# Seven block products for three pairs of feed-forward groups per stage

## The chip, the cores and the metric

The kernel runs on one core of one Trainium2 chip, as one program. The metric is the device time in microseconds: the median of three runs was 724.07 us (723.87 to 724.22). In the profile TensorE is PE (its weight loads PEld), VectorE is DVE, ScalarE is ACT, GpSimd is POOL and SyncE, which issues most DMAs, is SP.

## The reference

Two transformer-like blocks run one after the other on 256 tokens of width 1024, all in float32. The first block has a gated linear recurrence and a block-causal attention; the second has a Fourier and convolution mixer, a pooling mixer, and after each of the two a gated feed-forward part. The change is in that part alone, which is computed twice (layer 0 and layer 1, called the first and second feed-forward stage here):

```python
def swiglu_ffn(h, w_gate, w_up, w_down):
    return (jax.nn.silu(h @ w_gate) * (h @ w_up)) @ w_down
# h: 256 x 1024, w_gate and w_up: 1024 x 2816, w_down: 2816 x 1024
x = x + swiglu_ffn(rmsnorm(x, norm_ffn_g_2[layer]), ...)
```

## The kernel before

**Numbers.** Each float32 operand of a big product is split into a high part in the format fp32r and the rest as a low part. `product` (L1638) then does three matmuls into one PSUM bank: high by high, high by low, low by high. Weights come from memory in slabs of 128 x 2048 floats (1 MB). For a slab, ScalarE copies the raw slab into the high part (`stream`, L665) and VectorE subtracts that from the raw slab to get the low part (L1068 is the helper that records every such two-operand instruction). There are five raw buffers and four split buffers (`NRAW`, `NSPL`).

**Tiling.** The 2816 hidden columns are 11 groups of 256. For a group i, gate and up columns stand side by side, 512 columns; two slabs cover the 8 blocks of 128 input rows (kt 0 to 3, kt 4 to 7). `gate_up` (L2042) does, for both halves a of the tokens (128 each) and 8 kt, three matmuls of 512 columns: 48. ScalarE applies silu with the row norm to the gate half (`gates`, L1002), VectorE multiplies it with the up half (`hidden`, L1071). TensorE turns the result (`turn_hidden`, four 128 x 128 transposes, L2064), ScalarE and VectorE split it (`hidden_high`, `hidden_low`), and `down` (L2068) multiplies it with one slab of w_down: 24 matmuls into four banks that are held for the whole stage.

**Order.** It is written by hand, one list for each engine, and each engine runs its list in order. TensorE's unit for group i is gate and up of i, turn of i − 1, down of i − 2. ScalarE and VectorE run their share of `stream` three slabs ahead of TensorE: `fill(k)` (L682, L1122) brings them to slab k + 3 (`LOOK`). A split buffer is free for slab k when TensorE is done with slab k − 4 (`before_split`, L525). The unit's list on both is: fill of its two slabs, gates or hidden of both token halves, the split of the turned group i − 1, fill of the down slab. The four remaining PSUM banks go round in a ring between gate and up results and turned groups. SyncE issues a slab's DMA when the raw buffer's slab five ahead of it has been split (`emptied`).

Of the kernel before, what the change touches and what calls it, by code (L numbers as in the profile page):

```python
# [6 lines left out]
P, T, D, KT = 128, 256, 1024, 8  # L7
# [5 lines left out]
STEPS = [step for i in range(NG) for step in [("gu", i)] + ([("d", i - 2)] if i >= 2 else [])]  # L13
STEPS += [("d", NG - 2), ("d", NG - 1)]
# [3 lines left out]
def slab_plan():  # L18
# [45 lines left out]
    for layer in range(2):  # L64
        if layer:
            plan.append(("heads", "pool_map_2", 0))
        for kind, i in STEPS:
            if kind == "gu":
                plan.extend(("gu", None, layer, k0, i) for k0 in (0, 4))
            else:  # L70
                plan.append(("down", "ffn_w_down_2", layer, i))
# [28 lines left out]
RING = [i for i in range(len(PLAN)) if i not in OWN]  # L100
MATS = [i for i in RING if PLAN[i][0] not in ("first", "mod")]
# [15 lines left out]
def slab_of():  # L117

    at, k = {}, 30
    for layer in range(2):  # L120
        if layer:
            at["pool"] = k
            k += 1
        for kind, i in STEPS:
            at[kind, layer, i] = k
            k += 2 if kind == "gu" else 1
    assert k == len(MATS)
    return at


AT = slab_of()


# [34 lines left out]
def outputs():  # L168
# [100 lines left out]
    for layer in range(2):  # L269
        held("d", layer)  # L270
        ring = 0

        def take(*names):
            nonlocal ring
            for x in names:
                o.place(4 + ring % 4, x)
                ring += 1

        for i in range(NG):
            two = run("gu", (layer, i, 0), (layer, i, 1))  # L280
            take(*two)
            if i == 0:
                turned(2 * layer, 1)
            o.finish(*two)
            o.slab(AT["gu", layer, i], None)
            o.slab(AT["gu", layer, i] + 1, two[1])
            if i:
                take(("ht", layer, i - 1))
                o.finish(("ht", layer, i - 1))
            if i >= 2:  # L290
                o.slab(AT["d", layer, i - 2], None)
        take(("ht", layer, NG - 1))
        o.finish(("ht", layer, NG - 1))
# [21 lines left out]

OUT = outputs()
# [20 lines left out]
def two_block_program(nc, w_d, vec_d, cst_d, dft_d, rcnt_d, row_d, x_d, out_d):  # L337
# [6 lines left out]
    with ctx:  # L344
# [17 lines left out]
        F0 = sb("f0", [P, 8 * 272])  # L362
        F1 = sb("f1", [P, 8, T])
# [34 lines left out]
        s_sum = {k: sem(f"s_sum{k}") for k in BY_DMA}  # L398

# [57 lines left out]
        prow, frow = acc[0], acc[1]  # L457

# [62 lines left out]

        def raw_of(i):
            return raw[RING.index(i) % NRAW]

# [9 lines left out]
        def freed(name):  # L534
# [38 lines left out]
            if kind == "gu":  # L573
                return s_hid, hid_at(*at)
            if kind == "ht":
                return s_glo, NG * i + at[1] + 1
# [6 lines left out]
        def hid_at(layer, i, a):  # L583
            return 2 * (NG * layer + i) + a + 1
# [4 lines left out]
        def _(e):  # L589
# [5 lines left out]
            n_mod = n_mat = 0  # L595
            emptied = []
            for i, slab in enumerate(PLAN):
                n = width(i)
                if i in OWN:
# [12 lines left out]
                else:  # L612
                    n_mat += 1
                    k = n_mat - 1
                    emptied.append((s_minus, BY_DMA.index(k) + 1) if k in BY_DMA else (s_lo, LOW_AT[k]))
                    if n_mat == 6:
# [9 lines left out]
        def _(e):  # L626
# [27 lines left out]
            e.dma_start(rc, rcnt_d).then_inc(s_rc, 16)  # L654
            e.dma_start(prow[:, :], row_d[0]).then_inc(s_prow, 16)
            e.wait_ge(s_cv3, 1)
            e.dma_start(frow[:, :], row_d[1]).then_inc(s_frow, 16)

        @block.scalar
        def _(e):  # L660
# [6 lines left out]
            def stream(upto):  # L667

                while at["plan"] <= upto:
# [6 lines left out]
                    p.wait_ge(*landed(i))  # L676
# [319 lines left out]
            def gates(layer, i):  # L996
                for a in range(2):
                    at_ = hid_at(layer, i, a)
                    p.wait_ge(*ended("gu", layer, i, a))
                    if at_ > 4:  # L1000
                        p.wait_ge(s_hid, at_ - 4)
                    e.activation(tt[(at_ - 1) % 4][:, :], bank_of("gu", layer, i, a)[:, 0:T], ACT.Silu,  # L1002
                                 scale=rn[:, 2 * layer, a:a + 1]).then_inc(s_sgt, 1)

# [9 lines left out]
            def ffn(layer):  # L1014
# [12 lines left out]
                for i in range(NG):  # L1027
                    k = AT["gu", layer, i]
                    fill(k)
                    fill(k + 1)  # L1030
                    gates(layer, i)
                    if i:
                        hidden_high(layer, i - 1)
                    if i >= 2:
                        fill(AT["d", layer, i - 2])
                hidden_high(layer, NG - 1)
# [26 lines left out]
        def _(e):  # L1063
# [41 lines left out]
            def stream(upto):  # L1105

                while at["plan"] <= upto:
# [12 lines left out]
                    tt_(w[:, 1, 0:n], raw_of(i)[:, 0:n], w[:, 0, 0:n].bitcast(f32), SUB).then_inc(s_lo, 1)  # L1120

# [423 lines left out]
            def hidden(layer, i):  # L1545
                for a in range(2):
                    at_ = hid_at(layer, i, a)
                    p.wait_ge(s_sgt, at_)
                    if i >= 2:
                        p.wait_ge(*ended("ht", layer, i - 2))  # L1550
                    stt(tt[4 + (at_ - 1) % 4][:, :], bank_of("gu", layer, i, a)[:, T:2 * T], rn[:, 2 * layer, a:a + 1],
                        tt[(at_ - 1) % 4][:, :], MUL, MUL).then_inc(s_hid, 1)

# [7 lines left out]
            def ffn(layer, *name):  # L1561
# [5 lines left out]
                for a in range(2):  # L1567
# [10 lines left out]
                for i in range(NG):  # L1578
                    k = AT["gu", layer, i]
                    fill(k)  # L1580
                    fill(k + 1)
                    hidden(layer, i)
                    if i:
                        hidden_low(layer, i - 1)
                    if i >= 2:
                        fill(AT["d", layer, i - 2])
                hidden_low(layer, NG - 1)
# [43 lines left out]
        def _(e):  # L1631
# [450 lines left out]

            def ffn(layer):
# [153 lines left out]
```

## Time and profile before

| | |
|---|---|
| median of three runs | 724.07 us |
| the profiled execution, its own time | 724.69 us |
| span in the profile (first to last instruction) | 722.9 us |
| mean granted TensorE clock | 0.994 of full speed |
| the two feed-forward stages, by the profile's times | about 329 to 515 us and 531 to 717 us |
| matmuls of 512 columns, mean of one (they overlap) | 389 to 395 ns, 1776 of them |
| slab splits: ScalarE copies, VectorE subtractions | 99 of 1913 ns, 95 of 2290 ns |
| HBM read | 156.74 MB |

The times of groups are busy times; matmuls overlap, so that the spacing of two of them is less than the duration of one. "Idle before" is the time in which the engine stood still ahead of an instruction, and the name behind the arrow is what ended it.

### The profile page before, as it was taken

What the parts mean: (1) busy time and instruction counts of PE and PEld (TensorE: products, weight loads), DVE (VectorE), ACT (ScalarE), POOL (GpSimd) and SP (SyncE); (2) the same over time, 40 slices, a digit from 0 to 9 for tenths busy, and PEclk for the clock granted to TensorE, in tenths of its full rate; (3) what the DMA queues carried; (4) which work ended last, traced back from release to release, by engine and by line L of the source; (5) the groups of instructions that cost most, each with busy time, mean ns of one, the idle gap of its engine ahead of it and who ended that gap; (6) DMA issues with size and microseconds to landing.
All of it is one profiled execution on the core that took longest, in us unless ns stands there. A gap on an engine that the chain in (4) does not pass through costs nothing.

```text
span 722.9 us, 9536 instructions
## 1 busy us (share of the span) xinstructions
PE 709.7 (98%) x3812; PEld 617.6 (85%) x3812; DVE 498.4 (69%) x799; ACT 397.1 (55%) x616; POOL 12.6 (2%) x18
## 2 busy tenths in 40 slices
PE   6999999999999999999999999999999999999996
PEld 5888889989999999888888888888888888888885
DVE  5789999798977889976754545545776455454544
ACT  3156536965775778778634444344755433444323
POOL 0000000000310001000000000000000000000000
PEclk8999999999999999999999999999999999999999
DMA  8999997599836359434755454555236554555101
GB/s 329 418 421 413 422 403 262 172 392 349 342 118 233 118 175 263 145 117 174 289 178 181 189 205 181 175 178 194 95 123 234 200 200 174 178 195 206 63 1 58
DMA packets 23469, 158.40 MB, mean 219 GB/s; under 512 B 2625, under 2 KB 2881, under 8 KB 5249
## 3 DMA queue, kind: packets, MB, share of 16 engines
q1 hardware_dynamic: 22464, 152.82, 56.4%
q0 software_dynamic: 960, 4.98, 2.5%
q8 instruction: 30, 0.49, 0.3%
q14 instruction: 15, 0.11, 0.0%
HBM read 156.74 MB, written 1.05 MB: 218 GB/s over the span
## 4 chain that ended last, share of the span: by engine, by line
PE 84%; DVE 9%; ACT 5%; DMA 1%; issue 1%; SPq 0%; DVEq 0%
PE pb L1640 21%; PE pb L1642 21%; PE pb L1641 21%; PE pb L1712 14%; DVE raw L1071 3%; DVE w L1068 3%; PE pb L1959 2%; PE pb L2064 1%; PE pb L2132 1%; ACT w L665 1%; PE pb L1987 1%; DMA x<-x_dram 1%; ACT t L783 1%; ACT r L780 1%; DVE r L1068 1%
## 5 line engine op out<-in xcount | busy, mean ns | idle before, releaser
L1068 DVE TENSOR_TENSOR w<-raw,w 128x2048 fp32r<-128x2048 f32 x95 | 216.9, 2290 | 142.8 <-ACT w L665 142.7
L665 ACT ACTIVATE w<-raw 128x2048 fp32r<-128x2048 f32 x99 | 188.5, 1913 | 144.6 <-PE pb L1642 114.7
L1640 PE MATMUL pb<-w,r 128*128 128x512 f32 (+1 forms) x608 | 238.8, 393 | 0.2 <-DVE r L1068 0.2
L1642 PE MATMUL pb<-w,r 128*128 128x512 f32 (+1 forms) x608 | 235.5, 387 | 0.0
L1641 PE MATMUL pb<-w,r 128*128 128x512 f32 (+1 forms) x608 | 235.0, 387 | 0.0
L1642 PEld LDWEIGHTS pb<-w,r 128*128 128x128 f32 x608 | 114.1, 188 | 23.8
L1640 PEld LDWEIGHTS pb<-w,r 128*128 128x128 f32 x608 | 114.2, 188 | 22.9 <-DVE r L1068 0.6
L1641 PEld LDWEIGHTS pb<-w,r 128*128 128x128 f32 x608 | 114.3, 188 | 22.3
L1640 PE MATMUL pb<-r,w 128*128 128x256 f32 x288 | 82.5, 287 | 0.3 <-DVE r L1068 0.3
L1642 PE MATMUL pb<-r,w 128*128 128x256 f32 x288 | 81.5, 283 | 0.0
L1641 PE MATMUL pb<-r,w 128*128 128x256 f32 x288 | 81.5, 283 | 0.0
L1071 DVE SCALAR_TENSOR_TENSOR raw<-raw,acc 128x1024 f32<-128x1024 f32 x64 | 75.1, 1219 | 4.4 <-DMA raw<-w_dram 4.4
L1712 PE MATMUL pb<-h,ow 128*128 128x256 f32 x256 | 56.6, 383 | 0.1
L1640 PEld LDWEIGHTS pb<-r,w 128*128 128x128 f32 x288 | 55.2, 192 | 0.8 <-DVE w L1068 0.7
L1712 PEld LDWEIGHTS pb<-h,ow 128*128 128x128 f32 x256 | 49.2, 193 | 7.4 <-issue 0.6
L1641 PEld LDWEIGHTS pb<-r,w 128*128 128x128 f32 x288 | 55.2, 192 | 0.1
L1642 PEld LDWEIGHTS pb<-r,w 128*128 128x128 f32 x288 | 55.2, 192 | 0.0
L1002 ACT ACTIVATE t<-pb,rn 128x256 f32<-128x256 f32 x44 | 20.7, 476 | 59.7 <-PE pb L1642 59.6
L1071 DVE SCALAR_TENSOR_TENSOR f<-f,vec 128x256 f32<-128x256 f32 x114 | 45.9, 476 | 0.1
L1071 DVE SCALAR_TENSOR_TENSOR t<-pb,rn,t 128x256 f32<-128x256 f32 x44 | 21.1, 482 | 22.8 <-ACT t L1002 22.8
L1712 PE MATMUL pb<-t,ow 128*128 128x256 f32 x128 | 27.8, 379 | 0.0
L1712 PEld LDWEIGHTS pb<-t,ow 128*128 128x128 f32 x128 | 24.3, 190 | 3.3
(215 smaller groups left out, 668.3 us busy)
## 6 DMA issues: line engine op xcount, KB each, us to landing
raw<-w_dram SPq DMA_DIRECT2D x129, 1024.0 KB, 4.9
ow<-w_dram SPq DMA_DIRECT2D x8, 1024.0 KB, 16.2
ow<-w_dram SPq DMA_DIRECT2D x8, 512.0 KB, 17.2
oh<-w_dram SPq DMA_DIRECT2D x2, 1024.0 KB, 22.1
w<-w_dram POOLq DMA_DIRECT2D x2, 1024.0 KB, 14.3
x<-x_dram SPq DMA_DIRECT2D x2, 512.0 KB, 5.7
f<-rc_dram POOLq DMA_DIRECT2D x1, 1024.0 KB, 5.1
acc<-row_dram POOLq DMA_DIRECT2D x2, 512.0 KB, 4.7
```

The source lines that it names most:

```text
L665: return e.activation(out, in_, ACT.Copy, **kw)
L780: e.activation(hi_of(R, kt), F3[:, kt, :], ACT.Identity, **kw).then_inc(done, 1)
L783: e.activation(tt[kt][:, :], F3[:, kt, :], ACT.Identity, **kw).then_inc(done, 1)
L1002: e.activation(tt[(at_ - 1) % 4][:, :], bank_of("gu", layer, i, a)[:, 0:T], ACT.Silu, scale=rn[:, 2 * layer, a:a + 1]).then_inc(s_sgt, 1)
L1068: return e.tensor_tensor(out, a, b, op)
L1071: return e.scalar_tensor_tensor(out, a, s, b, op0, op1, **kw)
L1640: e.matmul(out, a_hi, b_hi, start=start, stop=False)
L1641: e.matmul(out, a_hi, b_lo, start=False, stop=False)
L1642: return e.matmul(out, a_lo, b_hi, start=False, stop=stop)
L1712: return e.matmul(out, slab[:, o:o + P], rhs, start=start, stop=stop)
L1959: done = e.matmul(out_of("cv", 3), dg[j % 8], G0[:, 3, j:j + T], start=j == 0, stop=j == 30)
L1987: done = e.transpose(bank_of("tx", n, a, m)[:, j * P:j * P + P], Xt[:, a, o:o + P], ident)
```

## The change

Groups 3 and 4, 6 and 7, 9 and 10 of each stage are computed in pairs by Winograd's form of Strassen's scheme: the tokens are cut into two halves, the 1024 input columns into two halves, and the two groups are the two halves of the columns, so that 8 block products become 7. Each product is a half of the input rows by 512 columns for 128 tokens, 4 kt of three matmuls: 12 matmuls.

- Weights: the seven right sides are B11 (slab `11`), B21 (slab `21`) and five that VectorE forms. `form_sums` adds raw slabs of 128 x 2048 in place: B11+B12 (`e`), that + B22 (`g`), B12+B22 (`f`), and `g` + B21 (`h`); `22` is B22 itself. Slab 11 is loaded into a tile of its own, `chain` (F2's place), in which e, g and h follow. Each of the seven is split like a slab. As many slabs are loaded as before.
- Left sides: per stage, VectorE forms four blocks of the normed input (`block_sides`, `block_mixes`), ScalarE and VectorE split them (`block_high`, `block_low`) into the tile MX, which lies over F0 and F1.
- Results: ScalarE copies product 11 out (`snap`), and VectorE makes the two groups' four token halves from the products by seven sums of 128 x 512 (`made_from`: c11, u2, t, u3, c22, c12, c21). Gates and hidden of a pair read these sums, in the order (i, first half), (i+1, second), (i+1, first), (i, second).
- TensorE's order in a pair (`two_groups`): 11, 21, e, turn of i − 1, g, down of i − 2, f, 22, down of i − 1, h. In the last pair h stands ahead of the down of i − 1, and both groups are turned in the middle of that down. After an inner pair, the next single group turns both groups in the middle of its own gate and up.
- The matrix for the pooling mixer (rc, 1 MB) is loaded by GpSimd's queue after the last h of the first stage, since F2 is `chain` until then.

```diff
+PAIRS = (3, 6, 9)
+UNITS_OF = [("two" if i in PAIRS else "one", i) for i in range(NG) if i - 1 not in PAIRS]
+SEVEN = ("11", "21", "e", "g", "f", "22", "h")
+LAST = [NG - 2, NG - 1] if UNITS_OF[-1][0] == "two" else [NG - 1]
+SUMS = ("c11", "u2", "t", "u3", "c22", "c12", "c21")
...
+            plan.append(("11", None, layer, 0, i))
+            plan.append(("part", None, layer, 0, i + 1))
+            plan.append(("21", None, layer, 4, i))
+            plan.append(("part", None, layer, 4, i + 1))
+            plan.extend(("form", name, layer, i) for name in ("e", "g"))
+            plan.append(("down", "ffn_w_down_2", layer, i - 2))
+            plan.extend(("form", name, layer, i) for name in ("f", "22"))
+            rest = [("down", "ffn_w_down_2", layer, i - 1), ("form", "h", layer, i)]
+            plan.extend(rest if i + 2 < NG else reversed(rest))
...
+            seven = {name: ("seven", layer, i, name) for name in SEVEN}
+            r0, r1, r2, r3 = ring
+            for name, bank in zip(SEVEN, (r0, r1, r2, r0, r1, r3, r0)):
+                if name == "g":
+                    o.place(r3, *hts)
+                    o.finish(*hts)
+                o.place(bank, seven[name])
+                o.finish(seven[name])
+                o.slab(AT[name, layer, i], seven[name])
+            o.slab(AT["d", layer, i - 2], None)
+            o.slab(AT["d", layer, i - 1], None)
+            ring[:] = [r2, r1, r3, r0]
...
+        def emptied_at(i):
+
+            kind, name, layer, *at_ = PLAN[i]
+            if kind == "part":
+                return s_lo, LOW_AT[AT["f" if at_[0] == 0 else "22", layer, at_[1] - 1]]
+            if kind == "21":
+                return form_made("h", layer, at_[1])
+            k = MATS.index(i)
+            return (s_minus, BY_DMA.index(k) + 1) if k in BY_DMA else (s_lo, LOW_AT[k])
...
+                        p.wait_ge(s_lo, LOW_AT[AT["h", slab[2], PAIRS[q % len(PAIRS) - 1]]])
+                    e.dma_start(chain, w_d[i, :, :]).then_inc(s_ch, 16)
+                    continue
...
             e.wait_ge(s_flo, 4)
-            e.dma_start(rc, rcnt_d).then_inc(s_rc, 16)
             e.dma_start(prow[:, :], row_d[0]).then_inc(s_prow, 16)
             e.wait_ge(s_cv3, 1)
             e.dma_start(frow[:, :], row_d[1]).then_inc(s_frow, 16)
+            e.wait_ge(s_lo, LOW_AT[AT["h", 0, PAIRS[-1]]])
+            e.dma_start(rc, rcnt_d).then_inc(s_rc, 16)
 
...
+            def block_high(layer):
+
+                for n, made in ((0, 5), (2, 6), (1, 7), (3, 8)):
+                    p.wait_ge(s_blk, 8 * layer + made)
+                    copy(mixes(n, 0), blocks[:, (1, 0, 2, 3)[n], :, :]).then_inc(s_bhi, 1)
+
+            def snap(layer, i):
+
+                p.wait_ge(*ended("seven", layer, i, "11"))
+                copy(snaps[:, 0, :], bank_of("seven", layer, i, "11")[:, :]).then_inc(s_snap, 1)
...
+                for kind, i in UNITS_OF:
+                    if kind == "two":
+                        k = AT["11", layer, i]
+                        fill(k)
+                        if i == PAIRS[0]:
+                            p.wait_ge(s_blo, 4 * layer + 4)
+                        snap(layer, i)
+                        fill(k + 1)
+                        fill(k + 2)
+                        gates(layer, i, [0])
+                        hidden_high(layer, i - 1)
+                        fill(k + 3)
+                        fill(k + 4)
+                        fill(k + 5)
+                        gates(layer, i + 1, [1])
+                        fill(k + 6)
+                        gates(layer, i + 1, [0])
+                        fill(k + 7)
+                        gates(layer, i, [1])
+                        fill(k + 8)
+                        continue
...
+            def form_sums(k, kind, name, layer, *at_):
+
+                g = at_[-1]
+                if kind == "11":
+                    top = part(layer, 0, g)
+                    p.wait_ge(*landed(top))
+                    p.wait_ge(s_lo, LOW_AT[k])
+                    tt_(chain, chain, raw_of(top)[:, :], ADD).then_inc(s_form, 1)
+                elif name == "e":
+                    top, low_ = part(layer, 0, g), part(layer, 4, g)
+                    p.wait_ge(*landed(low_))
+                    p.wait_ge(s_lo, LOW_AT[k])
+                    tt_(chain, chain, raw_of(low_)[:, :], ADD).then_inc(s_form, 1)
+                    p.wait_ge(*form_made("e", layer, g))
+                    tt_(raw_of(top)[:, :], raw_of(top)[:, :], raw_of(low_)[:, :], ADD).then_inc(s_form, 1)
+                elif name == "22":
+                    own_ = PLAN.index(("21", None, layer, 4, g))
+                    p.wait_ge(s_lo, LOW_AT[AT["g", layer, g]])
+                    tt_(chain, chain, raw_of(own_)[:, :], ADD).then_inc(s_form, 1)
...
+            def block_sides(layer, a):
+
+                p.wait_ge(s_rlo, split_at(2 * layer, a, 7))
+                for n, kt in ((0, 0), (3, 4)) if a == 0 else ((2, 0), (1, 4)):
+                    x = R1[:, kt:kt + 4, :, a * P:a * P + P].bitcast(f32)
+                    tt_(blocks[:, n, :, :], x[:, :, 0, :], x[:, :, 1, :], ADD).then_inc(s_blk, 1)
+
+            def block_mixes(layer):
+
+                def made(n):
+                    p.wait_ge(s_blk, 8 * layer + n)
+
+                a11, a22, a21, a12 = (blocks[:, n, :, :] for n in range(4))
+                made(4)
+                tt_(a22, a21, a22, SUB).then_inc(s_blk, 1)
+                made(5)
+                tt_(a21, a11, a21, SUB).then_inc(s_blk, 1)
+                made(6)
+                tt_(a11, a22, a11, SUB).then_inc(s_blk, 1)
+                made(7)
+                tt_(a12, a12, a11, ADD).then_inc(s_blk, 1)
+
+            def block_low(layer):
+
+                for m, n in enumerate((0, 2, 1, 3)):
+                    p.wait_ge(s_bhi, 4 * layer + m + 1)
+                    tt_(mixes(n, 1), blocks[:, (1, 0, 2, 3)[n], :, :][:, :, :], mixes(n, 0).bitcast(f32),
+                        SUB).then_inc(s_blo, 1)
+
+            def made_from(layer, i, name, *others):
+
+                product_, at_, x, y, op = {
+                    "c11": ("21", 1, None, 0, ADD), "u2": ("g", 0, None, 0, ADD), "t": ("e", 2, None, 0, SUB),
+                    "u3": ("f", 0, None, 0, ADD), "c22": ("f", 3, 2, None, SUB), "c12": ("22", 2, None, 2, ADD),
+                    "c21": ("h", 0, None, 0, ADD)}[name]
+                p.wait_ge(*ended("seven", layer, i, product_))
+                p.wait_ge(s_snap, pair_at(layer, i) + 1)
+                for other in others:
+                    p.wait_ge(s_fork, fork_at(layer, i, other))
+                x, y = (bank_of("seven", layer, i, product_)[:, :] if z is None else snaps[:, z, :] for z in (x, y))
+                tt_(snaps[:, at_, :], x, y, op).then_inc(s_fork, 1)
...
+                    if a:
+                        block_sides(layer, 0)
...
+                block_sides(layer, 1)
                 fill(29 if layer == 0 else AT["pool"] + 1)
                 for a in range(2):
                     norm_close(n, a)
-                for i in range(NG):
+                block_mixes(layer)
+                for kind, i in UNITS_OF:
+                    if kind == "two":
+                        k = AT["11", layer, i]
+                        fill(k)
+                        fill(k + 1)
+                        made_from(layer, i, "c11")
+                        fill(k + 2)
+                        hidden(layer, i, [0])
+                        hidden_low(layer, i - 1)
+                        fill(k + 3)
+                        made_from(layer, i, "u2", "c11")
+                        fill(k + 4)
+                        made_from(layer, i, "t", "u2")
+                        fill(k + 5)
+                        made_from(layer, i, "u3", "t")
+                        made_from(layer, i, "c22", "t")
+                        fill(k + 6)
+                        hidden(layer, i + 1, [1])
+                        made_from(layer, i, "c12", "c22")
+                        fill(k + 7)
+                        hidden(layer, i + 1, [0])
+                        made_from(layer, i, "c21", "u3")
+                        hidden(layer, i, [1])
+                        fill(k + 8)
+                        continue
...
+                    if i == 1:
+                        block_low(layer)
...
+            def seven(layer, i, name):
+
+                k = AT[name, layer, i]
+                w = W[(k + 2) % NSPL]
+                n = {"e": 0, "g": 1, "f": 2, "22": 3}.get(name)
+                bank_free("seven", layer, i, name)
+                weights(k)
+                if n is None:
+                    kt0, a = {"11": (0, 0), "21": (4, 0), "h": (4, 1)}[name]
+                    hi, lo = (R1[:, kt0:kt0 + 4, h, a * P:a * P + P] for h in range(2))
+                else:
+                    p.wait_ge(s_blo, 4 * layer + 4)
+                    hi, lo = mixes(n, 0), mixes(n, 1)
+                for j in range(4):
+                    o = j * 512
+                    done = product(bank_of("seven", layer, i, name)[:, :], hi[:, j, :], lo[:, j, :], w[:, 0, o:o + 512],
+                                   w[:, 1, o:o + 512], j == 0, j == 3)
+                done.then_inc(s_ps, 1)
+
+            def two_groups(layer, i):
+
+                for name in ("11", "21", "e"):
+                    seven(layer, i, name)
+                turn_hidden(layer, i - 1)
+                seven(layer, i, "g")
+                for c in range(2):
+                    down(layer, i - 2, c, range(2))
+                for name in ("f", "22"):
+                    seven(layer, i, name)
+                if i + 2 < NG:
+                    for c in range(2):
+                        down(layer, i - 1, c, range(2))
+                    seven(layer, i, "h")
+                    return
+                seven(layer, i, "h")
+                down(layer, i - 1, 0, range(2))
+                for j in LAST:
+                    turn_hidden(layer, j)
+                down(layer, i - 1, 1, range(2))
+
             def ffn(layer):
-                for i in range(NG):
-                    if i:
+                for kind, i in UNITS_OF:
+                    if kind == "two":
+                        two_groups(layer, i)
+                        continue
+                    hts = turned_in(kind, i)
+                    if len(hts) == 2:
+                        gate_up(layer, i, range(0, 4), range(2))
+                        for j in hts:
+                            turn_hidden(layer, j)
+                        gate_up(layer, i, range(4, 8), range(2))
...
```

## Rows read from the trace of the kernel before

**Rows 1.** The page, part 1: busy us, share of span, instructions.

```profile
PE 709.7 (98%) x3812; PEld 617.6 (85%) x3812; DVE 498.4 (69%) x799; ACT 397.1 (55%) x616; POOL 12.6 (2%) x18
```

**Rows 2.** Waits of TensorE, whole run: us in total, times, longest.

```profile
PE pb L1733 <- DVE f L1068: 4.6, 1, 4.6
...
PE pb L1640 <- DVE r L1068: 0.5, 2, 0.3
```

**Rows 3.** The chain of waits: start us, us, engine, line, count.

```profile
352.37 0.44 PE pb L2064 x4
...
380.56 0.44 PE pb L2064 x4
...
397.37 0.44 PE pb L2064 x4
```

**Rows 4.** Timeline around a feed-forward unit's end: start us, us, engine, line, instruction.

```profile
590.24 0.39 PE L1640 MATMUL pb<-w,r 128*128 128x512 f32 x1
...
597.04 0.39 PE L1640 MATMUL pb<-w,r 128*128 128x512 f32 x1
...
598.40 0.60 PE L2064 MATMUL pb<-cst,t 128*128 128x128 f32 x4
...
598.60 0.48 ACT L1002 ACTIVATE t<-pb,rn 128x256 f32<-128x256 f32 x1 [0.20 <-PE pb L1642]
...
599.04 0.60 ACT L665 ACTIVATE r<-pb 128x512 fp32r<-128x512 f32 x1
...
599.53 1.91 ACT L665 ACTIVATE w<-raw 128x2048 fp32r<-128x2048 f32 x1
...
601.47 2.29 DVE L1068 TENSOR_TENSOR w<-raw,w 128x2048 fp32r<-128x2048 f32 x1 [1.11 <-ACT w L665]
```

**Rows 5.** Groups by form: busy us, mean ns of one, idle before, releaser.

```profile
L1068 DVE TENSOR_TENSOR w<-raw,w 128x2048 fp32r<-128x2048 f32 x95 | 216.9, 2290 | 142.8 <-ACT w L665 142.7
L665 ACT ACTIVATE w<-raw 128x2048 fp32r<-128x2048 f32 x99 | 188.5, 1913 | 144.6 <-PE pb L1642 114.7 <-DMA raw<-w_dram 26.8 <-DVE rn L1542 3.1
...
L1068 DVE TENSOR_TENSOR r<-pb,r 128x512 fp32r<-128x512 f32 x22 | 15.2, 692 | 8.6 <-ACT r L665 7.1
...
L665 ACT ACTIVATE r<-pb 128x512 fp32r<-128x512 f32 x22 | 13.2, 600 | 8.9 <-PE pb L2064 8.9
```

**Rows 6.** Busy us of each engine in one feed-forward unit (window table).

```profile
398.00:415.00 17.00, 17.00 (x79) 14.04 (x78) 8.72 (x7) 7.34 (x7) 0.00 (x0) 1.00 0.49 184
```

**Rows 7.** Timeline of VectorE and ScalarE alone, instructions that follow each other.

```profile
341.63 4.49 DVE L1068 TENSOR_TENSOR w<-raw,w 128x2048 fp32r<-128x2048 f32 x2 [2.05 <-ACT w L665]
...
346.04 0.87 DVE L1071 SCALAR_TENSOR_TENSOR t<-pb,rn,t 128x256 f32<-128x256 f32 x2
...
531.98 1.28 DVE L1068 TENSOR_TENSOR x<-pb,x 128x512 f32<-128x512 f32 x2
...
710.05 0.69 DVE L1068 TENSOR_TENSOR x<-pb,x 128x512 f32<-128x512 f32 x1 [2.88 <-PE pb L1642]
710.78 0.69 DVE L1068 TENSOR_TENSOR f<-x,acc 128x512 f32<-128x512 f32 x1
...
345.37 3.72 ACT L665 ACTIVATE w<-raw 128x2048 fp32r<-128x2048 f32 x2
```

**Rows 8.** Timeline of VectorE at the first feed-forward stage's start.

```profile
334.18 2.16 DVE L1071 SCALAR_TENSOR_TENSOR r<-pb,vec,r 128x128 fp32r<-128x128 f32 x8 [0.87 <-ACT r L988]
...
352.24 0.48 DVE L1071 SCALAR_TENSOR_TENSOR t<-pb,rn,t 128x256 f32<-128x256 f32 x1 [0.42 <-ACT t L1002]
```

**Rows 9.** Windows at the kernel's start; PEclk is the granted TensorE clock.

```profile
10.00:11.00 1.00, 0.00 (x0) 0.00 (x0) 0.90 (x2) 0.00 (x0) 0.00 (x0) 1.00 0.99 381
11.00:12.00 1.00, 0.48 (x3) 0.48 (x3) 0.97 (x3) 0.00 (x0) 0.00 (x0) 0.50 1.02 426
17.00:18.00 1.00, 1.00 (x5) 0.79 (x4) 0.96 (x5) 0.00 (x0) 0.00 (x0) 0.58 1.08 447
```

**Rows 10.** The page, part 6: DMA issues, KB each, us to landing.

```profile
raw<-w_dram SPq DMA_DIRECT2D x129, 1024.0 KB, 4.9
```

More of the change, by code:

```diff
@@ L99 @@
 OWN = [i for i, p in enumerate(PLAN) if p[0] in ("u", "g", "y") or p[0] == "heads" and p[1] != "pool_map_2"]
-RING = [i for i in range(len(PLAN)) if i not in OWN]
-MATS = [i for i in RING if PLAN[i][0] not in ("first", "mod")]
+RING = [i for i in range(len(PLAN)) if i not in OWN and PLAN[i][0] not in ("11", "form")]
+MATS = [i for i in range(len(PLAN)) if i not in OWN and PLAN[i][0] not in ("first", "mod", "part")]
 MODS = [i for i in RING if PLAN[i][0] == "mod"]
@@ L270, in outputs @@
         held("d", layer)
-        ring = 0
+        ring = list(FIRST_RING)
         def take(*names):
-            nonlocal ring
             for x in names:
-                o.place(4 + ring % 4, x)
-                ring += 1
-        for i in range(NG):
[L280 to L286, printed above, removed]
-            if i:
[L288 to L293, printed above, removed]
+                o.place(ring.pop(0), x)
+                ring.append(o.bank[x])
+        for kind, i in UNITS_OF:
+            hts = run("ht", *((layer, j) for j in turned_in(kind, i)))
+            if kind == "one":
+                two = run("gu", (layer, i, 0), (layer, i, 1))
+                take(*two)
+                if i == 0:
+                    turned(2 * layer, 1)
+                take(*hts)
+                if len(hts) == 2:
+                    o.slab(AT["gu", layer, i], None)
+                    o.finish(*hts, *two)
+                else:
+                    o.finish(*two, *hts)
+                    o.slab(AT["gu", layer, i], None)
+                o.slab(AT["gu", layer, i] + 1, two[1])
+                if i >= 2:
+                    o.slab(AT["d", layer, i - 2], None)
[9 more added lines that the diff above has]
+                o.slab(AT[name, layer, i], seven[name])
+            o.slab(AT["d", layer, i - 2], None)
+            o.slab(AT["d", layer, i - 1], None)
+            ring[:] = [r2, r1, r3, r0]
+        take(*run("ht", *((layer, j) for j in LAST)))
+        o.finish(*run("ht", *((layer, j) for j in LAST)))
         o.finish(("d", layer, 0, 0), ("d", layer, 0, 1), ("d", layer, 1, 0))
@@ L361, in two_block_program @@
         X = sb("x", [P, KT, T])
-        F0 = sb("f0", [P, 8 * 272])
-        F1 = sb("f1", [P, 8, T])
+        with ExitStack() as over:
+            F0 = over.enter_context(nc.sbuf_tensor("f0", [P, 8 * 272], f32))
+            F1 = over.enter_context(nc.sbuf_tensor("f1", [P, 8, T], f32))
+        MX = sb("mx", [P, 8 * 272 + 8 * T], f32r)
         F2 = sb("f2", [P, 8, T])
@@ L574, in freed @@
                 return s_hid, hid_at(*at)
+            if kind == "seven":
+                if at[2] == "11":
+                    return s_snap, pair_at(i, at[1]) + 1
+                last = {"21": "c11", "g": "u2", "e": "t", "f": "c22", "22": "c12", "h": "c21"}[at[2]]
+                return s_fork, fork_at(i, at[1], last)
             if kind == "ht":
@@ L2184 @@
             continue
-        if p[0] == "gu":
+        if p[0] == "form":
+            continue
+        if p[0] in ("gu", "11", "21", "part"):
             _, _, layer, k0, g = p
```

156 lines of the change are left out of this document (116 added, 40 removed).

## Prediction, on record before the changed kernel ran

> **What bounds the kernel now.** I read the page first: TensorE is busy over 98% of the span, VectorE 69%, ScalarE 55% [rows 1]. The waits say that this is real work: TensorE's one long wait is at the start, and behind it stand tenths [rows 2]. The chain of waits then shows the regular feed-forward unit (a group's gate and up products, a turn, an older group's down products): turns at 380.56 and 397.37, so 16.81 us per unit [rows 3]. In the timeline 30 matmuls of 512 columns take 597.04 − 590.24 = 6.80 us, 0.2267 us each [rows 4]. A unit's 72 are 16.32 us, and the turn is the other 0.49. In such a unit VectorE works 8.7 us of 17, ScalarE 7.3 [rows 6]: TensorE sets the pace and VectorE has about 8 us to spare per group.
>
> **Durations.** Splitting a slab is a ScalarE copy of 1.91 and a VectorE subtraction of 2.29; on 512 columns they are 0.60 and 0.69 [rows 5]. Back to back they start closer: two subtractions take 4.49, so 2.20 from start to start; two of 512 columns 1.28, so 0.6; two of 256 0.87, so 0.39; ScalarE's copies 3.72, so 1.81 [rows 7]. An instruction that waits for the one ahead starts 0.03 to 0.04 after its end (710.05 + 0.69, next 710.78) [rows 7], and so does one that waits for the other engine (601.47 behind 599.53 + 1.91) [rows 4].
>
> **What TensorE saves.** A pair needs 7 products of 12 matmuls where it had 8 × 12: 12 × 0.2267 = 2.72 us. Six pairs: 16.3 us. Turns and down products stay. The products keep 512 columns and three matmuls in a row to one bank, as now, so I take the same 0.2267. No row shows a weight read from the new tiles; with weight loads hidden now, I bound that cost by 0 and 5% (0.8 us per stage) and take 0.
>
> **What VectorE gets.** A pair has 9 slab splits (7 products, 2 downs) instead of 6, four sums of 128x2048, seven block sums of 512, and its 4 gated halves and 2 lows as before. With the unit after it: 12 × 2.20 + 4 × 2.20 + 2 × 0.13 for sums that wait for their split + 7 × 0.6 + 6 × 0.4 + 3 × 0.6 = 44 us. TensorE needs 132 × 0.2267 + 0.5 for the pair and 72 × 0.2267 + 1.0 for the unit: 47.7 us. No row shows an in-place f32 sum; nearest are the subtraction of that size, 2.20 to 2.33 with a wait, and I take 2.20. So by busy time it just fits. It must then be asked whether VectorE may run without a hole, and this the new order forbids.
>
> **Three holes per pair.** Each engine runs its list in order. ScalarE's has the gate of (i+1, second half) ahead of the copy for slab k+9, the gate of (i+1, first half) ahead of k+10, and the gate of (i, second half) ahead of k+11. These gates wait for VectorE's block sums c22, c12, c21. VectorE asks for the same three slabs' low parts right after them. At c22 it stands for gate 0.44 + copy 1.92 + hops: the low part starts 3.1 after c22 starts, instead of 0.6. The same at c12. At c21 it waits 0.6 for the gate, makes the half, and waits 1.5 more for the copy. 7 us of holes: 44 + 7 = 51 us against TensorE's 47.7. VectorE is the bound in the pairs.
>
> **Inner pairs, walked.** Let 0 be the pair's start on TensorE. The unit ahead ends 5.93 before it (turn 0.49, down 5.44); from TensorE's turn to the next low part are 601.47 − 598.40 = 3.07 us [rows 4], so low e starts at −2.85. Then starts on VectorE: sum g −0.5, sum f 1.7, low g 3.9, low down 6.1, c11 8.3, low f 8.9, half 11.1, hidden low 11.5, low 22 12.1, sum h 14.3, u2 16.5, low down 17.1, t 19.3, low h 19.9, u3 22.1, c22 22.7, low 25.8, half 28.0, c12 28.4, low 31.5, half 33.7, c21 34.1, half 35.3, low down 37.2. TensorE asks for g at 8.7, the down at 11.4, f at 16.9, 22 at 19.6, the second down at 22.3, h at 27.7, the unit's first slab at 30.5: all there, the least reserve 2.4. But in the unit behind the pair VectorE has low 11 at 39.4, sum e at 41.7, and only then the hidden low of group i, ended 44.6. TensorE wants it for down(i) at 30.5 + 10.9 + 1.0 = 42.35. Stall 2.3 us behind pair 3. Pair 6 is entered with VectorE 0.9 later relative to TensorE (low e at −1.97), so 3.15 behind it. Two stages: 10.9 us. Bounds: 0 if VectorE had no holes; with each step at its full duration, 4 us each, 16.
>
> **The stage's end.** Pair 9 is entered at −1.97. Its order has h at once after 22, and behind h only half a down (2.72 us) before both groups are turned: TensorE is at the turn's second half at 28.0. VectorE: sum h 15.2, u2 17.4, low h 19.4 (it waits for ScalarE's copy), t 21.6, low down(8) 22.2, u3 24.4, c22 25.0, low down(9) 28.1, half 30.3, c12 30.7, low down(10) 33.8, half 36.0, c21 36.4, gate, the half of group 9 ended 38.1. Stall 10.15 us, in each stage: 20.3. Bounds: the chain behind h's end alone (c21, gate, half: 1.9 us) lies under the 2.72, so 0 from below; with full durations 12 from above.
>
> **The clock.** TensorE idled 4.6 us from 6.9 [rows 2]; its granted clock was 1.00 until 11.0, then 0.50 (the 1.2 GHz level), 4.1 us into the idle time, and back in the window of 17 to 18, at 17.84, 6.3 us after work began again at 11.52 [rows 9]. The idle 10 us at each stage's end are longer than those 4.1, so I expect it twice: 6.3 us at half speed lose 3.15, together 6.3 (bounds 0 and 6.3). The 2 to 3 us behind the inner pairs are shorter; no row shows what such a gap does, and between 0 and 3.15 each I take 0. The Trainium skill, "TensorE: Matmul & The Clock Gate", A second HAM failure mode, speaks against that 0: short idles that come often can throttle the clock as well. By it the sum could be up to 4 × 3.15 = 12.6 higher.
>
> **Stage starts.** The two first side sums lie in VectorE's wait for ScalarE's high parts (0.87 idle behind a copy and a small sum) [rows 8]. The two others come after the low parts ended at 336.34 (334.18 + 2.16), 0.6 later for the split behind them; then four chained mixes of 0.73. The low parts that started at 341.63 [rows 7] start at 343.0. ScalarE's four block copies (0.5 each) put the copies of 345.37 to 348.0, and the low parts behind them end at 354.35; the first half of group 1 then ends at 354.85 instead of 352.72 [rows 8]. TensorE wants its bank at 352.37 + 0.44 + 3 × 0.227 = 353.5 [rows 3]: 1.35 us. In the second stage the ring is a slab further at this point, and I take 0 (bound 1.35). The block lows after it lie in the units' spare 8 us.
>
> **DMA.** 1 MB lands in 4.9 us [rows 10]. The slabs kept longest are freed by low f, low 22 and sum h; the tightest, the unit's second slab, is freed at 16.6 and lands at 21.5, its copy starts at 29.5. The late load of the pool matrix is issued at the last low h, over 20 us before its use. Cost 0; a late slab would cost its delay.
>
> **Sum.** −16.3 + 1.35 + 10.9 + 20.3 + 6.3 = +22.5 us. The profiled execution took 724.69 (span 722.9); it gives 747.2. Against the median of 724.07, 0.6 less, 746.6.
>
> **Rivals.** (1) ScalarE isn't held up (its copies run ahead of the gates): no holes, VectorE's 44 us fit. Then only the stage end's 4.4 us stalls remain (half ended at 32.4 against 28.0), at the edge of the clock's fall: −16.3 + 1.4 + 8.8 = −6.1, 718. For it: copies need only their slab and buffer. Against it: the lists are in order. (2) TensorE stays the bound everywhere: 724.07 − 16.3 = 707.8. For it the 98% now; against it 44 of 47.7 us. (3) The holes are as told but the clock doesn't fall: 740.3. Against it the kernel's start. (4) VectorE's steps don't overlap at all: each starts after the full duration of the one ahead, 0.09 more on some 25 steps per cycle, 2.2 us in each of six places (four inner, two ends), 13 more, about 760. Against it 4.49 for two [rows 7]. The Trainium skill, "VectorE: DVE Perf Modes", The DRAIN you can't avoid, states just that, that the next operation waits until the pipe is empty. By it the sum is 13 higher. The row of 4.49 contradicts it for operations that wait for nothing.
>
> **Chances.** Forecast 0.72, (3) 0.10, (4) 0.05, (1) 0.09, (2) 0.04. By the ends of the terms I put 80% between 736 and 752: the clock costing nothing and shorter stalls below, full durations in part above. 0.2% (1.5 us) is about what can be told from no change. Faster 0.12 (both first rivals, less their slow side), same 0.03, slower 0.85.
>
> **What would show it.** Right: no wait of TensorE in the pairs themselves; waits of 2 to 3 us for the hidden low part (r) in the units of groups 5 and 8; two of about 10 us ahead of a turn, for the last gated half; a granted clock of 0.5 behind each; VectorE idle before slab splits behind c22 and c12 with ScalarE as releaser, 2.5 us each. Wrong: TensorE waiting for slab low parts (w) inside a pair, for DMA, or an even spacing with a 2.72 us gain per pair.

## The result and the profile after

The changed kernel took 747.08 us (median of 4 runs, 746.26 to 748.17) against 724.14 us before: a ratio of 1.032 (95% interval 1.030 to 1.034). The forecast was 746.6. The profiled execution took 748.17 us with a span of 746.4, 23.5 more than the span before; the other three had spans of 744.5 to 745.3 at a slightly higher mean clock (0.976 to 0.979 against 0.972).

The page's part 1 and the clock's row (tenths of full speed in 40 equal slices of the span), which answer to [rows 1]:

```profile
PE 702.4 (94%) x3740; PEld 610.0 (82%) x3740; DVE 624.4 (84%) x907; ACT 434.9 (58%) x648; POOL 12.6 (2%) x18
...
PEclk8999999999999999999999999996999999999968
```

The waits of TensorE over the whole run (us in total, times, longest), which answer to [rows 2]:

```profile
PE pb L2333 <- DVE t L1241: 20.1, 3, 9.9
PE pb L1909 <- DVE r L1238: 9.5, 6, 2.5
PE pb L2002 <- DVE f L1238: 5.0, 1, 5.0
PE pb L1909 <- DVE t L1241: 1.4, 1, 1.4
```

L2333 is the turn of a gated group; it waits for the last gated half, 9.9 us at each stage's end, and once for 0.3. L1909, the first matmul of a product, waits for r, the hidden low part, behind the inner pairs (2.4, 2.5, 2.4 and 1.6 us), and once for t, the gated half that keeps its bank, at the first stage's start. There are 72 fewer matmuls, and none waits for a slab's low part (w) inside a pair. VectorE is busy 84% of the span.

VectorE in pair 3, which TensorE begins at 371.62, from the last block sum of product f (c22) on (start us, us; in brackets the idle time ahead and what ended it):

```profile
394.37 0.68 DVE L1238 TENSOR_TENSOR f<-f,pb 128x512 f32<-128x512 f32 x1
397.43 2.29 DVE L1238 TENSOR_TENSOR w<-raw,w 128x2048 fp32r<-128x2048 f32 x1 [2.38 <-ACT w L796]
...
400.04 0.68 DVE L1238 TENSOR_TENSOR f<-pb,f 128x512 f32<-128x512 f32 x1
403.11 2.29 DVE L1238 TENSOR_TENSOR w<-raw,w 128x2048 fp32r<-128x2048 f32 x1 [2.38 <-ACT w L796]
...
406.97 0.49 DVE L1241 SCALAR_TENSOR_TENSOR t<-f,rn,t 128x256 f32<-128x256 f32 x1 [0.58 <-ACT t L1134]
408.77 2.29 DVE L1238 TENSOR_TENSOR w<-raw,w 128x2048 fp32r<-128x2048 f32 x1 [1.32 <-ACT w L796]
```

ScalarE in the same stretch:

```profile
395.08 0.51 ACT L1134 ACTIVATE t<-f,rn 128x256 f32<-128x256 f32 x1 [4.47 <-DVE f L1238]
395.50 1.90 ACT L796 ACTIVATE w<-raw 128x2048 fp32r<-128x2048 f32 x1
400.76 0.51 ACT L1134 ACTIVATE t<-f,rn 128x256 f32<-128x256 f32 x1 [3.36 <-DVE f L1238]
401.17 1.90 ACT L796 ACTIVATE w<-raw 128x2048 fp32r<-128x2048 f32 x1
```

Read the two together. ScalarE stands 4.47 us in front of a gate whose input, c22, VectorE makes at 394.37; only then does it copy the slab, though the copy needs nothing of c22. VectorE, done with c22, stands 2.38 us for the copy. The pair repeats it at c12, and in a shorter form at c21. That is the circle that the prediction read out of the two lists: 2.38 + 2.38 + 0.58 + 1.32 = 6.7 us of holes, where it had 7. Its walk through the pair holds to 0.1 us: it put c22 at 22.7 and the low part of slab 11 in the unit behind the pair at 39.4, and they start at 394.37 and 410.98, 22.75 and 39.36 behind the pair's start.

TensorE at the first stage's end, and its windows (length in us, busy us of PE, PEld, DVE, ACT and POOL, then the granted clock, the DMA engines' busy share and GB/s):

```profile
500.64 0.38 PE L2333 MATMUL pb<-cst,t 128*128 128x128 f32 x2
510.94 1.54 PE L2333 MATMUL pb<-cst,t 128*128 128x128 f32 x6 [9.91 <-DVE t L1241]
```

```profile
502.00:504.00 2.00, 0.00 (x0) 0.00 (x0) 2.00 (x3) 0.00 (x0) 0.00 (x0) 0.84 1.01 426
504.00:506.00 2.00, 0.00 (x0) 0.00 (x0) 0.16 (x1) 1.80 (x2) 0.00 (x0) 0.50 0.91 311
...
516.00:517.00 1.00, 1.00 (x4) 0.71 (x4) 0.00 (x0) 0.00 (x0) 0.00 (x0) 0.50 0.97 377
517.00:518.00 1.00, 1.00 (x6) 0.83 (x5) 0.00 (x0) 0.23 (x1) 0.00 (x0) 0.99 0.99 418
```

The two transposes of the first half run at 500.64, the others wait until 510.94. The granted clock falls to 0.50 (1.2 GHz) within the wait, in the window of 502 to 504, and stays there until 517.0. So 6.1 us of work run at half speed and lose 3.05; in the second stage 5.7 us, 2.85.

The difference of the two spans can be added up from the starts of the same TensorE instructions in both traces. A restart behind a wait adds 0.15 to 0.25 us to the idle time shown. The first stage is taken from its first turn to the first transpose of x behind it (L1987 before, L2256 after: 352.21 to 512.68, and 352.63 to 525.41), the second from the transposes of x ahead of it to its last matmul (533.47 to 716.36, and 546.20 to 739.74). Up to the first stage +0.4, in code that the change leaves alone; first stage −8.2 (36 matmuls of 0.2267) + 1.6 (start) + 2.6 + 3.0 (behind pairs 3 and 6) + 10.1 (the wait at the end) + 3.05 (the half clock behind it) = +12.2, measured 172.78 − 160.47 = +12.3; second stage −8.2 + 2.6 + 1.8 + 10.1 + 2.85 + 1.7 (a half clock behind an inner wait, below) = +10.9, measured 193.54 − 182.89 = +10.65; tail +0.1. Together +23.6 of 23.5.

### The profile page after: what moved, and what is told of

It is laid out like the page before. It is cut to its first block, busy times and chain, and to the rows that moved or that the text cites. A ratio compares the mean times of both kernels' runs of the same rounds, so it can differ in the third digit from the quotient of the medians.

```text
span 746.4 us, 9615 instructions
## 1 busy us (share of the span) xinstructions
PE 702.4 (94%) x3740; PEld 610.0 (82%) x3740; DVE 624.4 (84%) x907; ACT 434.9 (58%) x648; POOL 12.6 (2%) x18
## 4 chain that ended last, share of the span: by engine, by line
PE 43%; DVE 36%; ACT 12%; issue 7%; DMA 1%; SPq 0%; DVEq 0%; ACTq 0%
DVE w L1238 19%; PE pb L1981 13%; PE pb L1909 8%; PE pb L1910 8%; PE pb L1911 7%; DVE f L1238 7%; ACT w L796 7%; DVE raw L1241 3%; PE pb L2228 2%; DVE t L1241 2%; DVE raw L1238 1%; DVE r L1238 1%; PE pb L2451 1%; DMA x<-x_dram 1%; ACT t L914 1%
## 5 line engine op out<-in xcount | busy, mean ns | idle before, releaser
L1238 DVE TENSOR_TENSOR w<-raw,w 128x2048 fp32r<-128x2048 f32 x89 | 202.6, 2286 | 55.2 <-ACT w L796 55.1
L1909 PE MATMUL pb<-w,r 128*128 128x512 f32 (+1 forms) x488 | 194.0, 397 | 10.6 <-DVE r L1238 9.2
L796 ACT ACTIVATE w<-raw 128x2048 fp32r<-128x2048 f32 x93 | 175.7, 1909 | 43.2 <-DMA raw<-w_dram 25.5
L1910 PE MATMUL pb<-w,r 128*128 128x512 f32 (+1 forms) x488 | 190.7, 391 | 0.0
L1911 PE MATMUL pb<-w,r 128*128 128x512 f32 (+1 forms) x488 | 190.6, 390 | 0.0
L1909 PEld LDWEIGHTS pb<-w,r 128*128 128x128 f32 x488 | 93.2, 191 | 31.4 <-issue 10.9
L1911 PEld LDWEIGHTS pb<-w,r 128*128 128x128 f32 x488 | 93.1, 191 | 19.4
L1910 PEld LDWEIGHTS pb<-w,r 128*128 128x128 f32 x488 | 93.3, 191 | 18.1
L796 ACT ACTIVATE w<-f 128x2048 fp32r<-128x2048 f32 x24 | 46.0, 1915 | 64.0 <-DVE f L1238 53.7
L1909 PE MATMUL pb<-r,w 128*128 128x256 f32 x288 | 82.5, 287 | 0.3 <-DVE r L1238 0.3
L1911 PE MATMUL pb<-r,w 128*128 128x256 f32 x288 | 81.5, 283 | 0.0
L1241 DVE SCALAR_TENSOR_TENSOR raw<-raw,acc 128x1024 f32<-128x1024 f32 x64 | 75.1, 1218 | 4.1 <-DMA raw<-w_dram 4.1
L1238 DVE TENSOR_TENSOR w<-f,w 128x2048 fp32r<-128x2048 f32 x24 | 54.8, 2284 | 5.0 <-ACT w L796 5.0
L1909 PEld LDWEIGHTS pb<-r,w 128*128 128x128 f32 x288 | 55.2, 192 | 0.8 <-DVE w L1238 0.7
L1911 PEld LDWEIGHTS pb<-r,w 128*128 128x128 f32 x288 | 55.2, 192 | 0.0
L1134 ACT ACTIVATE t<-f,rn 128x256 f32<-128x256 f32 x24 | 12.2, 510 | 73.5 <-DVE f L1238 73.5
L1241 DVE SCALAR_TENSOR_TENSOR f<-f,vec 128x256 f32<-128x256 f32 x114 | 45.9, 474 | 0.1
L1238 DVE TENSOR_TENSOR f<-f,raw 128x2048 f32<-128x2048 f32 x18 | 41.2, 2290 | 1.3
```

The lines of the kernel that those rows point to most:

```text
L796: return e.activation(out, in_, ACT.Copy, **kw)
L1134: e.activation(tt[(at_ - 1) % 4][:, :], both_[:, 0:T], ACT.Silu, scale=rn[:, 2 * layer, a:a + 1]).then_inc(s_sgt, 1)
L1238: return e.tensor_tensor(out, a, b, op)
L1241: return e.scalar_tensor_tensor(out, a, s, b, op0, op1, **kw)
L1909: e.matmul(out, a_hi, b_hi, start=start, stop=False)
L1910: e.matmul(out, a_hi, b_lo, start=False, stop=False)
```

## The experiments

Each kernel ran beside the kernel before on the same chip. In the changed kernel L796 is what L665 was, L1134 L1002, L1238 and L1241 L1068 and L1071, L1909 to L1911 L1640 to L1642, L2333 L2064; in the last three kernels L1909 is L1924, L1238 and L1241 are L1245 and L1248, L2002 is L2017.

**Gates behind the copies.** ScalarE's list in a pair:

```diff
                         fill(k + 5)
-                        gates(layer, i + 1, [1])
                         fill(k + 6)
-                        gates(layer, i + 1, [0])
+                        gates(layer, i + 1, [1])
                         fill(k + 7)
-                        gates(layer, i, [1])
+                        gates(layer, i + 1, [0])
                         fill(k + 8)
+                        gates(layer, i, [1])
```

> On ScalarE the gates of (i+1, second half), (i+1, first half) and (i, second half) stand behind the copies for slabs k+9, k+10 and k+11 instead of ahead of them; nothing else changes. Theory (the order makes VectorE wait three times per pair): the waits of 2.4, 2.4 and 1.3 us of VectorE for those copies go, the stalls of 1.6 to 2.5 us behind pairs 3 and 6 go, and the stall at each stage's end falls from 9.9 to about 4.4 us: 747.1 - 9 - 11 - (0 to 6 for the clock) = 721 to 727, and 718 by the sum made before. Rival (VectorE has too much to do, whatever the order): the stalls stay within 1 us each and the time above 740 us.

Measured: 723.66 us, ratio to before 0.998 (0.996 to 0.999). VectorE behind pair 3, then TensorE's waits over the run:

```profile
394.00 0.68 DVE L1238 TENSOR_TENSOR f<-f,pb 128x512 f32<-128x512 f32 x1
394.59 2.28 DVE L1238 TENSOR_TENSOR w<-raw,w 128x2048 fp32r<-128x2048 f32 x1
396.80 0.48 DVE L1241 SCALAR_TENSOR_TENSOR t<-f,rn,t 128x256 f32<-128x256 f32 x1
397.19 0.68 DVE L1238 TENSOR_TENSOR f<-pb,f 128x512 f32<-128x512 f32 x1
397.79 2.28 DVE L1238 TENSOR_TENSOR w<-raw,w 128x2048 fp32r<-128x2048 f32 x1
```

```profile
PE pb L2333 <- DVE t L1241: 8.5, 2, 4.3
```

The low part now starts 0.6 us behind c22 instead of 3.06. The inner waits are gone altogether, and the end's wait is 4.3 us (4.4 expected). The place of three lines cost 23 us. The rival, that the amount of VectorE's work does it, falls here. What remains is the end: 2 × 4.3 and the clock, which fell to 0.50 at both and stayed there for 3.2 and 5.7 us of work, a loss of 4.4 us:

```profile
500.00:502.00 2.00, 2.00 (x7) 1.61 (x7) 2.00 (x3) 0.79 (x2) 0.00 (x0) 0.50 0.90 377
...
700.00:702.00 2.00, 2.00 (x7) 1.52 (x6) 0.56 (x1) 0.00 (x0) 0.00 (x0) 0.50 0.00 0
```

**Pairs 3 and 6 alone.**

```diff
-PAIRS = (3, 6, 9)
+PAIRS = (3, 6)
```

> Only groups 3, 4 and 6, 7 are paired; 9 and 10 are single groups as before. Theory (most of the loss stands at the stage's end): 2 x 2.7 us of matmuls come back, 2 x 9.9 us of stall and about 6 us of half clock go: 747.1 + 5.4 - 19.8 - 5.9 = 726.8 us. Rival (each pair costs the same): a third of the whole loss goes, 747.1 - 23/3 = 739.4 us.

Measured: 722.89 us, ratio 0.998 (0.997 to 0.999). Most of the loss does stand at the end, and the rival falls. But the time is 3.9 us below the expectation. The waits of TensorE in this kernel between 370 and 420 us (behind pair 3), and between 440 and 490 (behind pair 6):

```profile
PE pb L1909 <- DVE r L1238: 2.4, 1, 2.4
```

```profile
PE pb L2333 <- DVE t L1241: 0.3, 1, 0.3
PE pb L1909 <- DVE r L1238: 0.2, 1, 0.2
```

The stall behind pair 6 is 0.5 and not 2.8 us. I had overlooked that the unit behind it no longer forms a sum for a next pair (2.3 us on VectorE ahead of the hidden low part). So that stall was not pair 6's alone: what stands ahead of the hidden low part in VectorE's list sets it. From turn to turn, less the 12 matmuls that this order has more, TensorE is 2.4 us faster here in the first stage and 1.9 in the second, where no wait is left: 4.3 together, 0.4 more than was missing.

**Pair 9 alone.**

```diff
-PAIRS = (3, 6, 9)
+PAIRS = (9,)
```

> Only groups 9, 10 are paired. Theory: 724.1 - 5.4 + 1.4 for the start of the first stage + 2 x 9.0 (the pair is entered 0.9 us earlier than behind other pairs) + 5.9 for the clock = 744.0 us. Rival (the loss at the end is made by VectorE's arrears from the pairs ahead): with no pair ahead the end's stall is gone, and the time is about 724.1 - 5.4 + 1.4 = 720 us.

Measured: 744.88 us, ratio 1.028 (1.026 to 1.029). TensorE's waits:

```profile
PE pb L2333 <- DVE t L1241: 18.6, 2, 9.3
```

With no pair ahead the end's wait is 9.3 us instead of 9.9: what VectorE is behind from the pairs ahead counts 0.6 of it (0.9 expected), the rest is made in the last pair itself.

**Unused matmuls in the wait.** In front of the two turns of the last pair:

```diff
+                bank_free("ht", layer, NG - 1)
+                for _ in range(30):
+                    e.matmul(bank_of("ht", layer, NG - 1)[:, :], R1[:, 0, 0, 0:P], R1[:, 0:2, 0, :], start=True, stop=True)
                 for j in LAST:
                     turn_hidden(layer, j)
```

> As the changed kernel, with 30 more matmuls of 512 columns (6.8 us at full clock) into a free bank just where TensorE waits 9.9 us at each stage's end, so that it is idle for about 3 us only; their result isn't used. Theory (the idle time lets the clock fall, and the half clock behind it costs about 3 us each time): the granted clock stays at 1.00 and the time is 747.1 - 5.9 = 741.2 us. Rival (the fallen clock is hidden by something else that is late): 747 us, as without them.

Measured: 745.34 us (ratio 1.028, 1.027 to 1.030), 1.7 less instead of 5.9. The 3.1 us that were left idle were enough for the clock to fall at both ends:

```profile
724.00:725.00 1.00, 1.00 (x4) 0.81 (x3) 0.00 (x0) 0.00 (x0) 0.00 (x0) 0.50 0.00 0
...
512.00:513.00 1.00, 1.00 (x5) 0.90 (x4) 0.72 (x1) 1.00 (x3) 0.00 (x0) 0.50 1.04 442
```

So this run didn't hold the clock up, as it was meant to. It did make the time at half clock shorter: behind the two waits 2.8 and 3.4 us of work ran at 0.50, instead of 6.1 and 5.7. That is 2.8 us less lost, and the span of the profiled run is 2.6 us shorter. With 43 matmuls:

> As the run with 30 unused matmuls at each stage's end, with 43 of them, 9.75 us, which fill the whole of TensorE's 9.9 us wait; there 3.1 us of idle time were left, and the clock still fell to 0.5 for 3.0 and 3.4 us. Theory (the fallen clock is worth 5.9 us of the change's loss): the granted clock stays at 1.00 behind both ends and the time is 747.1 - 5.9 = 741.2 us. Rival (the time behind the wait is set by something else than the clock): as with 30, 745.3 us.

Measured: 743.72 us (ratio 1.027, 1.025 to 1.028), 3.4 less than the changed kernel in the medians, 4.5 in the spans of the profiled runs. Behind both ends, as in

```profile
512.00:514.00 2.00, 2.00 (x11) 1.62 (x11) 1.53 (x1) 1.40 (x3) 0.00 (x0) 1.00 0.62 262
```

the clock stays at 1.00. The fallen clock therefore cost time. Between the same landmarks, the second stage is 2.8 us shorter, the whole of its 2.85, and the first 1.7 of its 3.05. In the first, a new wait of 0.7 us for the hidden low part of group 9 appears, which the slow matmuls had covered. The medians differ by less than the profiled spans because the changed kernel's other runs had a higher mean clock than the profiled one (0.976 to 0.979 against 0.972). Each of the two profiles has one more fall behind an inner wait, in different stages, so the numbers are good to a few tenths.

**The last pair's order.** VectorE's and ScalarE's lists, in the last pair only:

```diff
                         made_from(layer, i, "c22", "t")
+                        if i + 2 == NG:
+                            made_from(layer, i, "c12", "c22")
+                            hidden(layer, i + 1, [1])
+                            made_from(layer, i, "c21", "u3")
+                            hidden(layer, i + 1, [0])
+                            hidden(layer, i, [1])
+                            fill(k + 6)
+                            continue
...
                         fill(k + 5)
+                        if i + 2 == NG:
+                            fill(k + 6)
+                            gates(layer, i + 1, [1])
+                            gates(layer, i + 1, [0])
+                            gates(layer, i, [1])
+                            fill(k + 7)
+                            continue
```

> Only the last pair's lists change. VectorE makes c22, c12, the half of group 10, c21, the other halves, and only then the low parts of the slabs of down(9) and down(10); ScalarE has the three gates ahead of the copy for down(10) and copies the next stage's slabs behind the turned groups. The inner pairs stay as changed. Theory: the last half is ended 28.5 us into the pair, where TensorE wants it at 28.0, so of 9.9 us of stall 0.5 are left and the clock stays up: 747.1 - 18.8 - 5.9 = 722.4 us. The inner stalls of 1.6 to 2.5 us stay. Rival (VectorE's amount of work sets the end, not its order): the low parts that are put off are late instead, and TensorE waits for them in down(9) and down(10) about as long; above 735 us.

Measured: 723.48 us, ratio 0.999 (0.998 to 1.000). The wait at each end is 0.4 us (0.5 expected). 23.6 us come back by what stands in the lists of one pair per stage; the low parts that were put off are late nowhere.

**Both orders, and the start.**

> The last pair's new lists together with ScalarE's gates behind the copies in the inner pairs. Theory: of all stalls only the 1.4 us (1.6 with the restart) at the first stage's start is left: 724.1 - 16.3 + 1.6 = 709.4 us. Rival (VectorE's 44 us of 47.7 per pair and unit don't fit once nothing else is late): new waits for slab low parts inside the pairs, above 713 us.

Measured: 709.94 us, ratio 0.980 (0.979 to 0.982). One long wait is left in the stages:

```profile
PE pb L1924 <- DVE t L1248: 1.4, 1, 1.4
```

The last edit takes that too:

```diff
-                    if i == 1:
-                        block_high(layer)
                     fill(k)
...
                     fill(k + 1)
+                    if i == 1:
+                        block_high(layer)
```

> As the run with both new orders, and ScalarE's four block copies of a stage stand behind the copies of group 1's two fills instead of ahead of them. Theory (they delay the low parts ahead of group 1's first half, for whose bank TensorE waits): the wait of 1.4 us in the first stage goes, the block sums are still in time for the first pair: 707.9 us, the full 16.3 us of the matmuls. Rival (the mixes on VectorE, not the copies, make it late): the wait stays above 1 us, 709 us.

Measured: 708.21 us, ratio 0.978 (0.976 to 0.979). Its page and its longest waits:

```profile
PE 693.8 (98%) x3740; PEld 605.5 (86%) x3740; DVE 623.5 (88%) x907; ACT 435.1 (62%) x648; POOL 12.2 (2%) x18
```

```profile
PE pb L2017 <- DVE f L1245: 3.2, 1, 3.2
PE pb L2001 <- DVE sq L1352: 1.3, 1, 1.3
PE pb L1924 <- DVE r L1245: 0.5, 2, 0.3
```

All that is left stands outside the pairs, mostly at the kernel's start. 724.46 − 708.21 = 16.25 us: the 16.3 of the 72 matmuls are all there. By start to start each stage is 8.4 us shorter than before. This version beats both kernels, with the same work on VectorE (623.5 us against 624.4) as the one that lost 23 us.

## Why the prediction was right

The mechanism is the one that was told, term by term. The closeness of the total (746.6 forecast, 747.1 measured) is in part luck, which the bullets on the inner stalls and the clock tell.

- **The matmuls' saving.** 2.72 us per pair and 0.2267 us each: the fastest version has the whole 16.3. Reading the new tiles costs nothing (weight loads 188 ns as elsewhere).
- **Three holes per pair.** 2.38, 2.38, 0.58 and 1.32 us measured, with the releasers that were named. Shown by the run with the gates behind the copies, which took out the holes and with them the inner stalls. The rival that ScalarE isn't held up had about the right price: with its condition made true, 718 plus the 4.4 us of half clock is 722.4, measured 723.7.
- **The inner stalls.** 2.3 and 3.15 forecast for each stage. By start to start 2.6 and 3.0 in the first stage, 2.6 and 1.8 in the second, where pair 6 was reached late because the clock had fallen before. In the runs with 30 and 43 matmuls and in the one with the last pair's order the smaller wait (1.6 to 1.7 us) stands in the same place, behind pair 6 of the stage in which the clock fell behind pair 3. 10.0 against 10.9.
- **The stage's end.** 10.15 forecast, 10.1 measured, twice. That the last pair's own lists make it is shown from both sides: pair 9 alone keeps 9.3 us of it, another order in that pair leaves 0.4.
- **The clock.** 6.3 forecast and 5.9 us seen as half speed behind the two ends in the profile; by the run without idle time it was worth about 3.4 to 4.5. The 3.15 of each end was the length of one fall, at the kernel's start, and that length isn't fixed: waits of 9.3 us in the run of pair 9 alone lost only 2.4 and 1.4 us. That 3.05 and 2.85 came so near is luck. The step that took 0 for the inner waits was wrong in the small: one of them in the profiled run was followed by 3.4 us at half clock, 1.7 us, of which some 1.2 came back, since the stall behind pair 6 was 1.8 instead of 3.0. The Trainium skill, "TensorE: Matmul & The Clock Gate", A second HAM failure mode, had warned of short idles that come often and throttle the clock. The trace agrees in part: one idle of 2.4 us did, but the inner waits stand over 50 us apart, and the other three were not followed by a fall. All half clock in the two stages of the profile is 1.3 us more than forecast (7.6 against 6.3), the inner stalls are 0.9 less; that these two nearly cancel is luck too.
- **The stage starts.** 1.35 forecast for the first, 1.4 of wait and 1.6 with the restart measured; 0 for the second, and none there. That ScalarE's block copies made it is shown by the last run.
- **DMA and the drain.** No wait for DMA in the stages. The rival in which VectorE's steps don't overlap (760 us) is refuted: in the gates run the instruction behind the low part at 394.59, 2.28 long, starts at 396.80, 2.21 later. The rule for it, in the Trainium skill, "VectorE: DVE Perf Modes", The DRAIN you can't avoid, doesn't hold for these; the same section says that an operation that isn't held starts earlier, which the prediction left out.

## What to carry to other kernels

Where two engines run fixed lists, write down for every instruction that waits for the other engine what stands behind it in its own list, and whether the other engine will ask for that. A busy sum that fits (44 of 47.7 us) doesn't show that the engine keeps up while such a circle is in its list; here three moved lines were worth 23 us and all the edits of the order 39. Put copies that depend on nothing new ahead of the instruction that waits, and at a stage's end let the chain that TensorE waits for go ahead of the slabs that it needs later.

## What the runs showed of the hardware

I had expected short waits of TensorE to leave its clock alone. Over the profiled runs of the changed kernel, of pairs 3 and 6, of both kernels with unused matmuls and of the last pair's order, there are fourteen inner waits of 2.4 to 2.6 us; at five of them the granted clock fell to 0.50 for 3.4 us, once in each run, now in the first stage, now in the second. In the changed kernel, behind the wait that ended at 628.2 us:

```profile
628.00:630.00 2.00, 1.77 (x7) 1.54 (x8) 2.00 (x3) 1.43 (x1) 0.00 (x0) 0.92 0.00 0
630.00:632.00 2.00, 2.00 (x6) 1.54 (x6) 2.00 (x4) 0.00 (x0) 0.00 (x0) 0.50 0.00 0
632.00:634.00 2.00, 2.00 (x8) 1.58 (x7) 1.90 (x2) 0.00 (x0) 0.00 (x0) 0.73 0.00 0
```

The fall comes 1.4 us after work has begun again. In three of the other four it comes 0.3 to 0.4 us after, in one (30 unused matmuls) 0.4 us before. In the same kernel the equal wait that ended at 416.4 had none behind it. None of the waits of 1.4 to 1.7 us had a fall, all of those of 3.1 us (two), 4.3 us (two) and 9 to 10 us (four) had one. What decides between two equal waits these runs don't show.

Nor is the moment or the length of a fall fixed. At the eight waits of 3.1 us and more, the clock fell between 2.0 and 5.4 us after TensorE had stopped (at one of the 3.1 us, 0.6 us after it had begun again); the prediction had taken the 4.1 us of one fall, at the kernel's start, as its measure. Work then ran at 0.50 for 2.8 to 6.1 us, and even two equal waits of one run differ: 4.8 and 2.9 us in the run of pair 9 alone. So one of these falls cost between 1.4 and 3.05 us.
